# Attention of a first block re-ordered (maxima first, keys on partitions), and the starts of a second block's stages split over three engines

## The reference, cut to what matters

```python
def gqa_attend(q, k, v):                      # q 256 tokens x 8 heads x 64
    def block(qb):
        s = jnp.einsum('bqkgd,bskd->bkgqs', qb, k).astype(jnp.float32) * scale
        p = jax.nn.softmax(s, axis=-1).astype(v.dtype)
        return jnp.einsum('bkgqs,bskd->bqkgd', p, v)
...
def rmsnorm_2(x, g):
    y = xf * lax.rsqrt(jnp.mean(xf * xf, axis=-1, keepdims=True) + EPS)
    return (y * g.astype(jnp.float32)).astype(x.dtype)
...
def half_ffn(h, shift, scale, gate, g_pre, g_post, w13, w2):
    u = modulate_2(rmsnorm_2(h, g_pre), shift, scale)          # x * (1 + scale) + shift
    return h + 0.5 * gate * rmsnorm_2(swiglu(u, w13, w2), g_post)
...
h_lat = half_ffn(h_lat, ...)                  # "fa"
h_lat = token_mixing(h_lat, ...)              # "mx", its output projection "wo2"
h_lat = half_ffn(h_lat, ...)                  # "fb"
```

## Time and profile before

| | |
|---|---|
| runs, us | 2486.65, 2491.21, 2491.04 (median 2491.04) |
| profiled execution | 2486.09 us, of which the span 2484.8 |
| mean granted TensorE clock | 0.905 |
| PE, DVE, ACT, POOL busy | 2044.4, 983.5, 744.1, 24.6 us |
| read from HBM | 669.12 MB |

### The profile page before, as it was taken

The page is one execution under the profiler, slowest core; times in us unless marked ns, Lnnn a source line. Parts: engine busy times, 40 slices in busy tenths (PEclk is TensorE's granted clock), DMA queues, the critical chain, the costliest instruction groups (busy, mean ns, idle before and its releaser), DMA issues.

```text
span 2484.8 us, 29409 instructions
## 1 busy us (share of the span) xinstructions
PE 2044.4 (82%) x12388; PEld 1356.7 (55%) x12388; DVE 983.5 (40%) x1697; ACT 744.1 (30%) x1194; POOL 24.6 (1%) x21
## 2 busy tenths in 40 slices
PE   5888777778778887777688799889889899889895
PEld 2534422333333333333344499669888798676684
DVE  2523412212122222123533344577655545553475
ACT  4333221111011111103110344534444544434444
POOL 0000000000000000000000000000000000000000
PEclk8979888998898899888899899989999899899897
DMA  8847799999999999999999855434345455330430
GB/s 353 353 162 297 278 405 414 410 409 410 411 412 407 410 409 410 409 402 410 399 408 411 287 177 173 147 101 137 94 146 168 136 178 174 131 102 9 144 111 17
DMA packets 228242, 672.08 MB, mean 270 GB/s; under 512 B 11520, under 2 KB 134528, under 8 KB 187792
## 3 DMA queue, kind: packets, MB, share of 16 engines
q1 hardware_dynamic: 228112, 670.21, 71.0%
HBM read 669.12 MB, written 1.05 MB: 270 GB/s over the span
## 4 chain that ended last, share of the span: by engine, by line
PE 54%; DMA 28%; DVE 11%; ACT 5%; issue 2%; POOL 0%; SPq 0%; DVEq 0%; ACTq 0%
DMA ring<-in_w 21%; PE pb L227 12%; PE pb L228 12%; PE pb L229 12%; DMA ring<-in_w_a 4%; PE pb L1470 3%; DVE WB L310 3%; PE pb L1493 2%; PE pb L578 2%; DMA ring<-in_w_in 1%; DMA ring<-in_w_mod 1%; PE pb L1454 1%; ACT WB L304 1%; DVE tmpT L414 1%; PE pb L755 1%
## 5 line engine op out<-in xcount | busy, mean ns | idle before, releaser
L310 DVE TENSOR_TENSOR WB<-ring,WB 128x1024 fp32r<-128x1024 f32 (+3 forms) x370 | 425.3, 1191 | 485.2 <-ACT WB L304 484.9
L304 ACT ACTIVATE WB<-ring 128x1024 fp32r<-128x1024 f32 (+3 forms) x370 | 361.2, 1025 | 776.6 <-DMA ring<-in_w_a 468.9
L227 PE MATMUL pb<-HH,WB 128*128 128x256 f32 (+1 forms) x1680 | 497.4, 296 | 15.7 <-DVE HL L2970 4.7
L228 PE MATMUL pb<-HL,WB 128*128 128x256 f32 (+1 forms) x1680 | 486.5, 290 | 0.0
L229 PE MATMUL pb<-HH,WB 128*128 128x256 f32 (+1 forms) x1680 | 485.7, 289 | 0.0
L1470 PE MATMUL pb<-ring,big 128*32 128x512 f32 x2048 | 297.3, 674 | 143.3 <-DMA ring<-in_w 125.8
L227 PEld LDWEIGHTS pb<-HH,WB 128*128 128x128 f32 x1680 | 332.5, 198 | 40.7 <-issue 18.6
L228 PEld LDWEIGHTS pb<-HL,WB 128*128 128x128 f32 x1680 | 332.7, 198 | 2.3 <-issue 2.2
L229 PEld LDWEIGHTS pb<-HH,WB 128*128 128x128 f32 x1680 | 331.8, 197 | 0.0
L1470 PEld LDWEIGHTS pb<-ring,big 128*32 128x32 f32 x2048 | 47.6, 114 | 358.7 <-DMA ring<-in_w 257.0
L1493 PE MATMUL pb<-ring,big 128*32 128x512 f32 x1024 | 175.1, 671 | 58.3 <-DMA ring<-in_w 50.5
(11 more groups left out here) (395 smaller groups left out, 1980.2 us busy)
## 6 DMA issues: line engine op xcount, KB each, us to landing
ring<-in_w SPq DMA_DIRECT2D x384, 1024.0 KB, 14.4
ring<-in_w_a SPq DMA_DIRECT2D x66, 1024.0 KB, 11.9
ring<-in_w_in SPq DMA_DIRECT2D x38, 1024.0 KB, 7.3
ring<-in_w_b SPq DMA_DIRECT2D x33, 1024.0 KB, 5.0
ring<-in_w_ada SPq DMA_DIRECT2D x32, 1024.0 KB, 6.5
ring<-in_w_mod SPq DMA_DIRECT2D x24, 1024.0 KB, 8.8
ring<-in_w_out SPq DMA_DIRECT2D x8, 1024.0 KB, 5.3
ring<-in_b_w_in SPq DMA_DIRECT2D x8, 1024.0 KB, 6.5
```

What stands on the lines that cost most here:

```text
L227: pe.matmul(o, l[0], r[0], start=start, stop=False)
L228: pe.matmul(o, l[0], r[1], start=False, stop=False)
L304: act.activation(WB[:, c % 2, 0, x:y], flat[:, x:y], ACT.Copy).then_inc(*A(("high", c, z)))
L310: dve.tensor_tensor(WB[:, c % 2, 1, x:y], flat[:, x:y], WB[:, c % 2, 0, x:y].bitcast(F32), ALU.subtract).then_inc(*V(("low", c, z), *([("f ...
```

## The change

For the attention, all 16 score products run first and DVE keeps only their minima, in one column each. PE transposes those to 8 rows, and products with a one-row pattern spread each head's minima over 128 partitions (`mbc`). In the loop over heads the scores are formed again, now with keys on partitions and tokens along the row; DVE subtracts the minima, ACT takes the exponential in place. There is no transpose of the weights. The value product uses the weights as the stationary operand and moves 64 columns of V and a column of ones, so the sum comes with it. Four heads are divided, transposed and split together.

For the second block, the norms of "xf", "fa", "mx" and "fb" go tile by tile. All 16 transposes of a start are issued at once into four banks of two slices. DVE evicts slices 0 to 5 and ACT 6 and 7 with four buffers, POOL forms the low parts of slices 0 to 5 and DVE those of 6 and 7. The first chunk of a feed-forward takes both 128-column halves per slice. The stage ends of "fa", "wo2" and "fb" multiply the rows by their factors on DVE while ACT sums squares, and DVE adds into `X`.

```diff
+    def pe_turn2(pe, name, xn):
+        for i in range(2):
+            pe.wait_ge(*at("xn", name, i))
+            for kk in range(8):
+                c = 256 * (kk % 2) + 128 * i
+                e = pe.transpose(PB[4 + kk // 2][:, c:c + 128], xn(i)[:, kk * 128:kk * 128 + 128], ident)
+                if i and kk % 2:
+                    e.then_inc(*P(("turn", name, kk // 2)))
+    def act_norm2(act, name, junk, x_from):
+        act_ready(act)
+        for i in range(2):
+            for w in x_from(i):
+                act.wait_ge(*at(*w))
+            s = st[:, 16 + i:17 + i]
+            act.wait_ge(*last("a"))
+            act.activation(junk[:, 0:D], X[:, i, :], ACT.Square, scale=1.0 / 32, accum_out=s).then_inc(*A())
+            act_root(act, ("norm", name, i), s)
+    def dve_norm2(dve, name, xn, i):
+        dve_rstd(dve, ("norm", name, i), st[:, 16 + i:17 + i])
+        dve.wait_ge(*last("v"))
+        dve.tensor_scalar(xn(i), X[:, i, :], st[:, 16 + i:17 + i], None, ALU.mult).then_inc(*V(("xn", name, i)))
...
+    def dve_turn2(dve, name, a, s):
+        for kk in range(6):
+            if kk % 2 == 0:
+                dve.wait_ge(*at("turn", name, kk // 2))
+            if kk >= 4:
+                dve.wait_ge(*at("XT", name, kk - 4))
+            dve.tensor_scalar(vT[:, kk % 4, :], turn2_bank(kk), a(kk), s(kk), ALU.mult, ALU.add).then_inc(*V(("turned", name, kk)))
+        for kk in (6, 7):
+            dve.wait_ge(*at("highT", name, kk))
+            dve.tensor_tensor(HL[:, kk, 0:256], vT[:, kk % 4, :], HH[:, kk, 0:256].bitcast(F32), ALU.subtract).then_inc(
+                *V(("XT", name, kk)))
+    def act_turn2(act, name, a, s):
+        for kk in range(8):
+            if kk < 6:
+                act.wait_ge(*at("turned", name, kk))
+            act.activation(HH[:, kk, 0:256], vT[:, kk % 4, :], ACT.Copy).then_inc(*A(("highT", name, kk)))
+            if kk in (3, 4):
+                act.wait_ge(*at("turn", name, 3))
+                act.wait_ge(*at("XT", name, kk - 1))
+                act.activation(vT[:, (kk + 3) % 4, :], turn2_bank(kk + 3), ACT.Identity, bias=s(kk + 3), scale=a(kk + 3)).then_inc(*A())
+            if kk == 5:
+                act.wait_ge(*last("a"))
+    def pool_turn2(pool, name):
+        for kk in range(6):
+            pool.wait_ge(*at("highT", name, kk))
+            pool.tensor_tensor(HL[:, kk, 0:256], vT[:, kk % 4, :], HH[:, kk, 0:256].bitcast(F32), ALU.subtract).then_inc(
+                *G(("XT", name, kk)))
...
+    def act_post2(act, name, banks):
+        act_ready(act)
+        for i in range(2):
+            act.wait_ge(*at("rows", name, i))
+            for j in (1, 0):
+                act.wait_ge(*last("a"))
+                if j == 0:
+                    act.wait_ge(*at("product", name, i, 0))
+                act.activation(tmp_row[:, 0:512], PB[banks[2 * i + j]][:, :], ACT.Square, scale=1.0 / 32,
+                               accum_out=st[:, 8 + 2 * i + j:9 + 2 * i + j]).then_inc(*A(("post", name, i, j)))
+            s = st[:, 8 + 2 * i:9 + 2 * i]
+            act.wait_ge(*at("eps", name, i))
+            act.wait_ge(*last("a"))
+            act.activation(st[:, i:i + 1], s, ACT.Sqrt, bias=st[:, 9 + 2 * i:10 + 2 * i]).then_inc(*A(("root", (name, i))))
+    def dve_post2(dve, name, row, banks, tmp, waits, ends):
+        for w in waits:
+            dve.wait_ge(*at(*w))
+        for i in range(2):
+            dve.wait_ge(*at("rows", name, i))
+            for j in range(2):
+                if j:
+                    dve.wait_ge(*at("post", name, i, 1))
+                    dve.tensor_scalar(st[:, 9 + 2 * i:10 + 2 * i], st[:, 9 + 2 * i:10 + 2 * i], 1e-6, None, ALU.add).then_inc(*V(("eps", name, i)))
+                dve.tensor_tensor(tmp[2 * i + j], PB[banks[2 * i + j]][:, :], row[:, 512 * j:512 * j + 512], ALU.mult).then_inc(
+                    *V(("product", name, i, j), *(ends if i and j else [])))
+            dve_rstd(dve, (name, i), st[:, i:i + 1])
+            dve.wait_ge(*last("v"))
+            for j in range(2):
+                x = X[:, i, 512 * j:512 * j + 512]
+                dve.scalar_tensor_tensor(x, tmp[2 * i + j], st[:, i:i + 1], x, ALU.mult, ALU.add).then_inc(*V(("added", name, i, j)))
...
-        run(pe_row(pe, "gt", pr[1][0], 5, [("kv_out", 3)]))
+        for n in range(16):
+            h, i = n // 2, n % 2
+            pl, r = h % 4, 64 * (h // 4)
+            if n >= 3:
+                pe.wait_ge(*at("mx1", n - 3))
+            else:
+                pe.wait_ge(*at(*(("kT", 3), ("qT", 1), ("kv_out", 3))[n]))
+            pe.matmul(PB[3 + n % 3][:, :], qT1[r:r + 64, pl, 128 * i:128 * i + 128], kT1[r:r + 64, :], start=True, stop=True).then_inc(
+                *P(("scores1", n)))
+        pe.wait_ge(*at("mx1", 15))
+        for i in range(2):
+            e = pe.transpose(PB[4][0:8, 128 * i:128 * i + 128], mxs[:, i, :], ident)
+        e.then_inc(*P(("m_turned",)))
+        run(pe_row(pe, "gt", gt_diag, 5, [("mx1", 14)]))
+        pe.wait_ge(*at("mT"))
+        for q in range(4):
+            if q >= 2:
+                pe.wait_ge(*at("mbc", q - 2))
+            elif q:
+                pe.wait_ge(*at("rowed", "gt", 1))
+            for z in range(2):
+                e = pe.matmul(PB[4 + q % 2][:, 256 * z:256 * z + 256], ident[0:8, 2 * q + z:2 * q + z + 1].to_broadcast([8, 128]), mT,
+                              start=True, stop=True)
+            e.then_inc(*P(("mb", q)))
...
         def scores(h):
             pl, r = h % 4, 64 * (h // 4)
+            for z in range(2):
+                if h >= 2:
+                    pe.wait_ge(*at("sub1", h - 2, z))
+                elif h + z == 0:
+                    pe.wait_ge(*at("gelu", 0, 0))
+                    pe.wait_ge(*at("mx1", 15))
+                for s_ in range(2):
+                    c = 256 * z + 128 * s_
+                    e = pe.matmul(PB[2 * (h % 2) + z][:, 256 * s_:256 * s_ + 256], kT1[r:r + 64, c:c + 128], qT1[r:r + 64, pl, :],
+                                  start=True, stop=True)
+                e.then_inc(*P(("scoresT1", h, z)))
+        def values(h):
+            steps(g2, 3)
+            if h == 0:
+                pe.wait_ge(*at("vaug"))
+                pe.wait_ge(*at("mbc", 2))
+                pe.wait_ge(*at("mbc", 3))
+            elif h == 4:
+                pe.wait_ge(*at("o_1", 0))
+            c = 65 * (h % 4)
             for i in range(2):
...
+                    if i == 0 and s_ % 2 == 0:
+                        pe.wait_ge(*at("p1", h, s_ // 2))
+                    e = pe.matmul(PB[4 + i][:, c:c + 65], pT1[h % 2][:, s_, 128 * i:128 * i + 128], vaug[:, s_, h // 4, :],
+                                  start=s_ == 0, stop=s_ == 3)
             e.then_inc(*P(("pv1", h)))
...
+        def o_turned(g):
+            pe.wait_ge(*at("o_1", g))
+            pe.wait_ge(*at("o1", 0) if g else at("gated", 1))
+            for c in range(2):
+                for i in range(2):
+                    x = 256 * g + 128 * c
+                    e = pe.transpose(PB[6][:, 256 * c + 128 * i:256 * c + 128 * i + 128], o_1[i][:, x:x + 128], ident)
+            e.then_inc(*P(("o_turned", g)))
...
+        for q in (0, 2):
+            act.wait_ge(*at("mb", q))
+            act.activation(mbc[:, 2 * q:2 * q + 2, :], PB[4 + q % 2][:, :].rearrange("p (h t) -> p h t", h=2), ACT.Copy).then_inc(*A(("mbc", q)))
+        def weights(h):
+            for z in range(2):
+                x = pT1[h % 2][:, 2 * z:2 * z + 2, :]
+                act.wait_ge(*at("sub1", h, z))
+                act.activation(x, x, ACT.Exp, scale=-1.0).then_inc(*A(("p1", h, z)))
+        def o_high(g):
+            act.wait_ge(*at("o_turned", g))
+            act.activation(HH[:, 2 * g:2 * g + 2, 0:256], PB[6][:, :].rearrange("p (c t) -> p c t", c=2), ACT.Copy).then_inc(*A(("o1_high", g)))
...
+        row = dve_row(dve, "gt", mcol1[:, 16:24, 0], gt_diag, [])
+        steps(row, 1)
+        for n in range(16):
+            dve.wait_ge(*at("scores1", n))
+            dve.tensor_reduce(mxs[:, n % 2, n // 2:n // 2 + 1], PB[3 + n % 3][:, :], AX, ALU.min).then_inc(*V(("mx1", n)))
+            if n == 2:
+                dve.wait_ge(*at("kp_turned", 3))
+                dve.memset(vaug[:, :, :, 64:65], 1.0).then_inc(*V())
+                dve.tensor_copy(vaug[:, :, :, 0:64], qkv[:, :, 640:768].rearrange("p s (z d) -> p s z d", z=2)).then_inc(*V(("vaug",)))
+        dve.wait_ge(*at("m_turned"))
+        dve.tensor_copy(mT, PB[4][0:8, 0:256]).then_inc(*V(("mT",)))
+        run(row)
+        for q in (1, 3):
+            dve.wait_ge(*at("mb", q))
+            dve.tensor_copy(mbc[:, 2 * q:2 * q + 2, :], PB[4 + q % 2][:, :].rearrange("p (h t) -> p h t", h=2)).then_inc(*V(("mbc", q)))
+        def weights(h):
+            for z in range(2):
+                dve.wait_ge(*at("scoresT1", h, z))
+                if h >= 2:
+                    dve.wait_ge(*at("pv1", h - 2))
+                elif z == 0:
```

(27 more changed lines are left out.)

173 lines of the change are left out of this document (65 added, 108 removed).

## The result

The changed kernel took 2471.22 us (median of 4 executions, 2470.23 to 2471.78) beside 2490.03 us for the kernel before on the same chip: ratio 0.9926, 95% interval 0.9913 to 0.9938, 18.8 us faster. The forecast was 2475 us and its range 2462 to 2486.

The account below looks back on a forecast made before the run. Bounds: waits between engines until about 300 us, then expert weights, from 1393 us TensorE's products with holes at stage starts. Savings 4.2 + 4.5 + 2.5 + 3.0 + 1.2 = 15.4 us gave 2470.7 to 2475.6; forecast 2475, range 2462 to 2486.

Parts of the forecast that it names:

- (a): First block's attention: 16 score products for the maxima, six at half clock and ten at full, 21.7 us, ending at 143.1.
- (b): Bridge from the last maximum to the first transposed score: transposes, gate-row and spreading products, 8.0 us, ending at 151.1.
- (c): Attention up to the end of head 7's scores: scores, values, loads, gating; 50.1 us, ending at 201.2.
- (d): Attention's tail to the output projection: wait at head 6, half clock behind it, last steps; 21.2 us, ending at 222.4.
- a microsecond saved ahead of the experts starts the weight stream earlier and is kept: Before the expert weights: any time saved there arrives in full at the kernel's end.
- the 4.2 us: First block's attention: total saving, output projection starting at 222.4 instead of 226.6.
- I take the same dozen microseconds here, so about 133: Maxima's products: TensorE's clock returns to full after about a dozen busy microseconds, as before, near 133 us.
- never in this part: Slow bound for the maxima's products: the clock does not return to full during them, costing 10 us more.
- Rival 2: Bridge's gaps pull the clock down, 5 us lost, plus 2 to 4 from GpSimd or loads: 2482 to 2486 us; chance 0.13.
- My own sign: Prediction is wrong if the clock from 121 to 222 averages under 0.75, or GpSimd's slices take over 0.8 us.
- 4.5 + 2.5 + 3.0 + 1.2: Savings in us at the starts of first feed-forward, mixer, second feed-forward and third block, in that order.
- 0.62 us a slice: Starts' slices: GpSimd's time for a low part of 256 columns, against 0.41 us on VectorE.

Follow-up runs that it names:

- no_maxima: The changed kernel without the 16 score products for the maxima, their reductions and spreading products; output not the reference's; 2448.84 us, ratio 0.984.
- early_rows: The changed kernel with ScalarE's copies of the second group's vector rows moved ahead of head 7's exponentials; 2471.74 us, ratio 0.9931.
- after_again: The changed kernel itself, measured once more for its spread; 2480.35 us, ratio 0.9959.
- attn_only: The kernel before with only the first block's new attention, the second block's stages old; 2495.57 us, ratio 1.0019.
- low_on_vector: The changed kernel with the six low parts of each start on VectorE instead of GpSimd; 2477.75 us, ratio 0.9947.

## Why the prediction came out, and where it was wrong

**Steps that held.** (a) and (b) in the profiled execution: 141.5 and 149.5 against 143.1 and 151.1; values took 2.00 us a head as taken. (c) ended at 201.3 against 201.2, but in part by luck: the clock fell near 149 and was back only near 159, which cost 4.6 us (first scores 7.19 us for two heads, three loads 4.10) that (c) did not have, and closer spacing and missing waits gave 2.9 us back; (b) had handed it 1.6 us. The price of a maximum product was a little high: I read 1.97 and 0.99 us from groups of four and two. In the run of 16, VectorE's reductions follow every 1.71 us at half and 0.86 us at full clock; why the products come closer here than in the group of four, 7.87 us at half clock, is not shown. (d) named the 3.76 us wait and the half clock behind it; the projection came at 223.45 instead of 222.4. Its two last waits (1.28 and 1.41 us) are the division and the split, both in the sum at 1.3; what was not in it is that the last three loads still ran mostly at half clock, 4.65 us instead of 2.8; shorter steps ahead of them gave 0.9 back. "fa": transposes 3.8 us earlier and slices done at 1408.8 against 1409.1. Transposes of the mixer: 6.7 us earlier in all, 7.0 forecast. Third block: its post step and start give 1.3 us, 1.2 forecast.

**The step that failed: "a microsecond saved ahead of the experts starts the weight stream earlier and is kept", as applied to the 4.2 us.** The rule is right in the large (no_maxima: 22.2 of 23.0 us kept). What I left out is that behind the new tail the clock falls at the projection's start, which the earlier trace rows could not show, as the old tail had one wait of 0.93 us there. It costs 2.7 to 4.0 us in each profile; that the waits at the tail are the cause is not tested. So the first block gave nothing here.

**The step behind it: "I take the same dozen microseconds here, so about 133".** I took the clock's return as a time that one row of before gives. It is a draw: at 135 in the profiled execution, behind 168 in early_rows. The bound of (a), "never in this part", came true in four of eight profiles. There the 16 products took 25.4 us, 4 more than the 21.7 of the sum and not 10, for at half clock one starts every 1.71 us and not every 1.97; in three of these four the whole bridge ran at half clock too, 13 us instead of 8.0. Rival 2 came true in after_again as it was put: full clock up to the bridge, half behind its first wait, and 5.1 us lost there. I gave it 0.13 and 2482 to 2486 us; three of the changed kernel's ten executions lie at 2482 to 2484, and of attn_only's 12, seven stand at 2494 to 2500 us, the others at 2487 to 2491. The cause that I named, the gaps, is not shown: the same gap passed at full clock in the other profile. My own sign says the same: the prediction was to be wrong if the clock from 121 to 222 averages under 0.75. It is 0.81 in the first profile and 0.74 in after_again, the same kernel. What decides over the clock here stays open.

**The term that was too small.** The second block gave 15.2 us where I had 4.5 + 2.5 + 3.0 + 1.2 = 11.2. "fa" and the mixer's start fit, 4.0 and 2.8 us; at "fa" the clock came back 8.5 us behind the first transpose, and 4.6 to 5.0 us in seven other profiles, where "fa" gives 5.6. 2.3 us came inside the mixer, where the clock stood at 0.97 instead of 0.92 from 1640 to 1700, which I had not counted and which other executions of the same starts do not all have (the stretch from the mixer's first square sum to that of "fb" is 325.7 to 329.1 us in them, 330.8 before). "fb" gave 4.8 us from the mixer's post step to its own (-9.1 to -13.8), 3.0 forecast: transposes 2.8 us earlier, the alternation 1.7, with the clock back 4.6 us behind the first transpose and not 8.4.

**GpSimd and the transposes.** I had 0.62 us a slice, from a pair of adds. The six slices of "fa", one by one (ns, least, median and most), and VectorE's two:

```profile
L611 POOL TENSOR_TENSOR HL<-tmpT,HH x6: 725/730/734, 1403.6 to 1407.5; 128x256 fp32r<-128x256 f32 x6
```

```profile
L593 DVE TENSOR_TENSOR HL<-tmpT,HH x2: 412/513/614, 1407.9 to 1408.4; 128x256 fp32r<-128x256 f32 x2
```

0.73 us against VectorE's 0.41 is 1.8 times, midway between my 1.5 and the Trainium skill's rule of about twice (GPSIMD Engine Reference, Engine selection). It made no difference to the time, as low_on_vector shows. The 0.6 us a start that I allowed for GpSimd and VectorE in each other's way came to 0.2: VectorE's first low part, which overlaps GpSimd's last, took 0.61 us at each of the three starts, the second 0.41. That transposes count as work for the clock, as I read rows 5, is borne out: in after_again the clock was back near 1412.5, when only the 16 transposes had run since 1408.49 and the first product was yet to start (1412.87).

The total was right by luck: 4.2 us too much at one place met 4.0 too little at another. By all ten executions (mean 2476.3 us) 2475 is a good figure for this kernel all the same, but for a sum that was not mine: nothing or a loss in the attention, 12 to 16 us in the second block.

## To carry to other kernels

Work that is added to TensorE in a stretch at half clock must be priced at both levels, and a clock that came back once in one trace is one draw; ask what the sum is if it does not. Read a lead at several landmarks down the line, not only where it arises, for the next stage can lose it again (3 us here, to a lower clock). A maximum that is only subtracted in a softmax need not be exact: rounded operands for it took the ratio from 0.9931 to 0.9907 here, and to 0.9888 with those that spread it rounded too. And three engines on a pipe help only if the third relieves the one that the others wait for; here TensorE waited for no slice, and the starts gained by beginning earlier.
